# One token block through attention, gated linear attention and pooling: where turned sums, a diagonal, a table load and two copies stand

## The reference, cut to what matters

```python
def first_block(x, ...):
    for l in range(DEPTH):                       # two layers
        h = rmsnorm(x, attn_norm_g[l])
        proj = h @ w_in[l]
        qa, ka, va, ga, cq, ckv, kr, gb = jnp.split(proj, SPLIT_POINTS, axis=-1)
        ya = swa_attention(...) * jax.nn.silu(ga)        # 16 heads, window 128
        yb = mla_attention(cq, ckv, kr, ...) * jax.nn.silu(gb)   # 8 heads, low-rank q and kv
        x = x + jnp.concatenate([ya, yb], axis=-1) @ w_out[l]
    return rmsnorm(x, final_norm_g)

def second_block(x, c, ctx, c_ctx, w_ada, ...):
    for i in range(DEPTH):
        sh, sc, gt = modulation(c_lat, w_ada[i], b_ada[i], 3)    # silu(c) @ w + b
        u = x * (1.0 + sc) + sh
        if i % 2 == 0:
            sh_c, sc_c = modulation(c_c, w_ada[i], b_ada[i], 2)
            uc = ctx_s * (1.0 + sc_c) + sh_c
            s_f, s_b = context_states(uc @ w_in_e[j][:, :E_STATE_COLS], ...)
            y, _, _ = even_mixer(u @ w_in_e[j], s_f, s_b, ...)   # 4 heads of gla_chunked, both directions
        else:
            y = odd_mixer(u @ w_in_o[j], w_pool[j], ...)
        x = layer_norm(alpha * x + gt * y, ln_g[i], ln_b[i])

def gate_log(r, w, b):
    return jax.nn.log_sigmoid((r @ w + b).astype(jnp.float32)) / GLA_TAU

def gla_chunked(q, k, v, log_a, s0):             # one head: decayed scores, decayed state
    g = jnp.cumsum(lac, axis=-2)
    decay = jnp.exp(jnp.where(lower, diff, -jnp.inf))
    scores = jnp.einsum('bhik,bhjk,bhijk->bhij', qc, kc, decay)
    o = (jnp.einsum('bhij,bhjv->bhiv', scores, vc)
         + jnp.einsum('bhik,bhkv->bhiv', qc * jnp.exp(g), s))
```

## Time and profile before

| what | value |
|---|---|
| three timed runs | 1691.81, 1695.49, 1695.62 us, median 1695.49 |
| the profiled execution's own time | 1694.16 us |
| its span, first to last instruction | 1692.4 us |
| PE busy | 1653.7 us, 98% |
| DVE busy | 1348.3 us, 80% |
| ACT busy | 903.3 us, 53% |
| transfers | 390.59 MB, mean 231 GB/s |
| granted TensorE clock, mean | 0.993 |

### The profile page before, as it was taken

One profiled execution on the slowest core, in us unless ns is written; L12 is line 12 of the kernel. 1 busy time (PEld: TensorE's weight loads), 2 busy tenths in 40 slices (PEclk: granted clock), 3 DMA queues, 4 the chain that ended last, 5 costly groups with the idle time before them and its releaser, 6 DMA issues.

```text
span 1692.4 us, 22024 instructions
## 1 busy us (share of the span) xinstructions
PE 1653.7 (98%) x7948; PEld 1372.3 (81%) x7948; DVE 1348.3 (80%) x1761; ACT 903.3 (53%) x1352; POOL 155.2 (9%) x222
## 2 busy tenths in 40 slices
PE   9999999999999999998999999999999999999996
PEld 8888888888888888786877878888877778888885
DVE  6988878879978878787975787778877978777766
ACT  6447564445475644655843466666534364444432
POOL 1100000001100000011211110000101101110000
PEclk9999999999999999999999999999999999999998
DMA  8965545658755546789987963434959869887663
GB/s 325 329 237 187 175 162 161 216 189 297 275 165 185 182 154 208 262 277 315 336 270 227 304 206 125 132 129 166 322 179 346 306 233 318 284 271 237 224 206 112
DMA packets 111409, 390.59 MB, mean 231 GB/s; under 512 B 16252, under 2 KB 17164, under 8 KB 109804
## 3 DMA queue, kind: packets, MB, share of 16 engines
q1 hardware_dynamic: 74944, 268.99, 45.6%
q0 software_dynamic: 27856, 101.19, 19.5%
q10 hardware_dynamic: 8510, 19.08, 3.2%
HBM read 385.02 MB, written 4.19 MB: 230 GB/s over the span
## 4 chain that ended last, share of the span: by engine, by line
PE 82%; DVE 7%; DMA 5%; ACT 3%; issue 2%; POOL 0%; ACTq 0%; DVEq 0%; SPq 0%; POOLq 0%
PE L L392 22%; PE L L393 22%; PE L L399 22%; DMA stage<-in_w_stream 5%; PE TP L505 3%; DVE wl L334 2%; PE AB L2506 2%; DVE macc L678 2%; PE AB L2203 1%; ACT wh L313 1%; PE TP L2216 1%; PE AB L2522 1%; PE AB L2440 1%; PE AB L2206 1%; PE AB L2229 1%
## 5 line engine op out<-in xcount | busy, mean ns | idle before, releaser
L392 PE MATMUL L<-wh,xth 128*128 128x512 f32 (+1 forms) x1948 | 783.6, 402 | 3.6 <-issue 2.7
L313 ACT ACTIVATE wh<-stage 128x1024 fp32r<-128x1024 f32 x504 | 530.5, 1057 | 476.2 <-PE L L399 336.4
L334 DVE TENSOR_TENSOR wl<-stage,wh 128x1024 fp32r<-128x1024 f32 x504 | 612.6, 1221 | 210.4 <-ACT wh L313 209.5
L393 PE MATMUL L<-wh,xtl 128*128 128x512 f32 (+1 forms) x1948 | 761.0, 391 | 0.0
L399 PE MATMUL L<-wl,xth 128*128 128x512 f32 (+1 forms) x1948 | 524.2, 390 | 1.8 <-DVE wl L334 1.7
L399 PEld LDWEIGHTS L<-wl,xth 128*128 128x128 f32 x1948 | 366.6, 188 | 79.5 <-DVE wl L334 3.1
L392 PEld LDWEIGHTS L<-wh,xth 128*128 128x128 f32 x1948 | 367.6, 189 | 77.5 <-issue 5.3
L393 PEld LDWEIGHTS L<-wh,xtl 128*128 128x128 f32 x1948 | 367.8, 189 | 73.5 <-issue 2.4
L678 DVE SCALAR_TENSOR_TENSOR macc<-mstage,scols,macc 128x1024 f32<-128x1024 f32 x240 | 306.9, 1279 | 7.3 <-DMA mstage<-in_w_mod 6.6
L745 POOL DMA_DIRECT2D mstage<-in_w_mod x192 | 138.9, 724 | 1256.4 <-DVE macc L678 1014.2
L815 ACT ACTIVATE pa<-pa,st 128x128 f32<-128x128 f32 x96 | 43.0, 450 | 67.9 <-DVE st L1403 37.4
(11 more groups left out here) (262 smaller groups left out, 1322.6 us busy)
## 6 DMA issues: line engine op xcount, KB each, us to landing
stage<-in_w_stream SPq DMA_DIRECT2D x504, 512.0 KB, 4.5
mstage<-in_w_mod POOLq DMA_DIRECT2D x192, 512.0 KB, 6.0
arena<-in_ctx ACTq DMA_DIRECT2D x1, 2048.0 KB, 9.4
x_kept<-X ACTq DMA_DIRECT2D x4, 512.0 KB, 7.5
X<-x_kept ACTq DMA_DIRECT2D x1, 2048.0 KB, 10.5
arena<-in_b_ada ACTq DMA_DIRECT2D x2, 1024.0 KB, 10.9
arena<-in_ln_g ACTq DMA_DIRECT2D x2, 1024.0 KB, 10.1
X<-in_x SPq DMA_DIRECT2D x3, 512.0 KB, 8.3
```

Of the source, the lines that this page charges most:

```text
L313: nc.scalar.activation(wh[:, s % SPLITS].rearrange("p a b -> p (a b)"), stage[:, s % RING, :], ACT.Copy).then_inc(hi_ready, 1)
L334: nc.vector.tensor_tensor(wl[:, s % SPLITS].rearrange("p a b -> p (a b)"), stage[:, s % RING, :], wh[:, s % SPLITS].rearrange("p a b -> p ...
L392: nc.tensor.matmul(dst[:, t, 0:width], xh, w, start=start and k == 0, stop=False, skip_group_check=True)
L393: nc.tensor.matmul(dst[:, t, 0:width], xl, w, start=False, stop=False, skip_group_check=True)
```

## The change

Seven places are touched; all of them change the order of work, and no product of the reference is computed otherwise.

1. In the last 16 slots of an attention layer PE turned x behind slots 6, 8, 10, 12 and the sums behind 7 and 9. Now x stands behind 6, 10, 14, 15 and the sums behind 8 and 12. ACT and DVE follow (8, 12, 16, 17; sums 10, 14).
2. The turned sums of the context stretch, behind its slot 23 before, stand behind the third latent slot and its gate. DVE's reductions move along. Two waits of PE on `mod_cols` go.
3. `head_gates(0)` stands behind the query slot 10, not 9; ACT's three steps on it and DVE's `decay_logs(0)` stand one step later too.
4. The first head's diagonal is summed by ACT behind the first level's exponentials and not ahead of slot step 4.
5. A one-element exponential on ACT stands between slot steps 4 and 5 of each head.
6. The first emptying of the low-rank query group waits for the third slot's first half alone (`first_queries`), not for the whole slot.
7. ACT's rounding of a gate row (`gate_row_high(0, 0)`, L963) stands behind one more slot copy.

```diff
@@ evac, evac_q: ACT in an attention layer
-                    slots_done(act, N0 + done)
+                    if done:
+                        slots_done(act, N0 + done)
+                    else:
+                        act.wait_ge(once("first_queries"), l + 1)
...
-                        evac_q(0, MIDQ + 3)
+                        evac_q(0, None)
@@ step: PE, third low-rank query slot
                                 last = products(L[(G0 + G_MIDQ + k) % 2], n % SPLITS, k, 2, False, lx)
+                                if k == 0:
+                                    last.then_inc(once("first_queries"), 1)
@@ last 18 steps of a layer: ACT
-                    if n in (8, 10, 12, 14):
-                        turn_x(l + 1, (n - 8) // 2)
+                    if n in (8, 12, 16, 17):
+                        turn_x(l + 1, (8, 12, 16, 17).index(n))
@@ the same: DVE
-                    if n in (8, 10, 12, 14):
-                        turn_x(l + 1, (n - 8) // 2)
-                    if n in (9, 11):
-                        mod_unit(1, (n - 9) // 2)
+                    if n in (8, 12, 16, 17):
+                        turn_x(l + 1, (8, 12, 16, 17).index(n))
+                    if n in (10, 14):
+                        mod_unit(1, (n - 10) // 4)
@@ the same: PE
-                    if n in (7, 9):
-                        turn_unit(1, (n - 7) // 2)
-                    if n in (6, 8, 10, 12):
-                        turn_x(l + 1, (n - 6) // 2)
+                    if n in (8, 12):
+                        turn_unit(1, (n - 8) // 4)
+                    if n in (6, 10, 14, 15):
+                        turn_x(l + 1, (6, 10, 14, 15).index(n))
@@ context stretch: DVE (on ACT "if n == 27: u.n += 2" goes, and u.n += 4 becomes 6)
-                if n == 27:
-                    mod_columns(dve, 4, 0, [u.take()[1], u.take()[1]], 2, 1, KT, True)
...
+                if n == 2:
+                    mod_columns(dve, 4, 0, [u.take()[1], u.take()[1]], 2, 1, KT, True)
@@ context and latent stretch: PE
-                if p == 23:
-                    turn_sums(0, 4, 0, [u.take()[1], u.take()[1]])
...
-                if j == 1:
-                    pe.wait_ge(mod_cols, MOD_COLS[5])
...
-                turned(pe, len(TURNS) + 2 + m + 1)
+                turned(pe, len(TURNS) + m + 1)
                 kv_step(m)
                 log_gate(m)
+                if m == 2:
+                    turn_sums(0, 4, 0, [u.take()[1], u.take()[1]])
...
-            pe.wait_ge(mod_cols, MOD_COLS[6])
@@ query stretch: PE; ACT's decay steps move from 10, 11, 12 to 11, 12, 13, DVE's from 13 to 14
-                if n == 9:
+                if n == 10:
                     low_rank_ready(2)
                     head_gates(0)
@@ a head's start: ACT
+                def diagonal_sums():
                     ...
+                if hd:
+                    diagonal_sums()
+                split_step(act, split_hi, R_G, HEAD_STEPS * hd + 4)
+                nc.scalar.activation(st[:, 52:53], ones[:, 0:1], ACT.Exp)
+                split_step(act, split_hi, R_G, HEAD_STEPS * hd + 5)
...
+                    if hd == 0 and v == 0:
+                        diagonal_sums()
@@ behind the heads: ACT
-            gate_row_high(0, 0)
-            split_pairs(act, split_hi, R_G + BESIDE, 1, evac_to(6144, 0, 1024))
+            split_pairs(act, split_hi, R_G + BESIDE, 1, evac_to(6144, 0, 1024),
+                        beside=lambda i, n: gate_row_high(0, 0) if n == 0 else None)
```

More of the change, by code:

```diff
@@ L999, in _ @@
                     keep_x((n - 24) // 4)
-                if n == 27:
-                    u.n += 2
                 if n >= 28:
@@ L1064, in _ @@
             z_uses = []
-            u.n += 4
+            u.n += 6
             def decay_abs(hd):
@@ L1091, in beside_q @@
                     low_rank_high(2)
-                if n == 10:
+                if n == 11:
                     decay_abs(0)
-                if n == 11:
+                if n == 12:
                     decay_exp(0)
-                if n == 12:
+                if n == 13:
                     decay_ln(0)
@@ L1122, in _ @@
                     split_step(act, split_hi, R_G, HEAD_STEPS * hd + n)
-                act.wait_ge(once("diagonal"), hd + 1)
-                for j in range(TT):
-                    d = pa[:, 1024 + GD * j:1024 + GD * j + GD]
-                    ins = nc.scalar.activation(d, d, ACT.Copy, accum_out=st[:, 54 + j:55 + j])
-                ins.then_inc(once("diagonal_sum"), 1)
-                for n in (4, 5):
-                    split_step(act, split_hi, R_G, HEAD_STEPS * hd + n)
+                def diagonal_sums():
+                    act.wait_ge(once("diagonal"), hd + 1)
+                    for j in range(TT):
+                        d = pa[:, 1024 + GD * j:1024 + GD * j + GD]
+                        ins = nc.scalar.activation(d, d, ACT.Copy, accum_out=st[:, 54 + j:55 + j])
+                    ins.then_inc(once("diagonal_sum"), 1)
+                if hd:
[3 more added lines that the diff above has]
+                split_step(act, split_hi, R_G, HEAD_STEPS * hd + 5)
                 for v, b in enumerate(LEVELS + [128]):
@@ L1674, in beside_q @@
                     gates_to_rows(2)
-                if n == 13:
+                if n == 14:
                     decay_logs(0)
```

## The result

The changed kernel took 1677.95 us (median of 4 runs, 1674.28 to 1678.49), the kernel before 1693.78 beside it (4 runs, 1691.81 to 1695.62). The ratio is 0.9906, with a 95% interval of 0.9886 to 0.9926: faster by 15.8 us, where 14.9 were forecast, and 1677.95 lies 1.6 us under the forecast 1679.5 and inside the range. A later comparison gave 0.9913 (0.9896 to 0.9929). The profiled execution took 1678.49 us, its span is 1676.7.

What follows compares the result with a forecast made beforehand. PE was taken as the bound, busy 1653.7 of 1692.4 us, leaving 38.7 us idle. Terms 6.3 + 2.2 + 1.8 + 3.5 + 0.8 + 0.3 = 14.9 from 1694.16 give 1679.3; forecast 1679.5 us, range 1672 to 1688.

Steps and rivals of the forecast that it cites:

- What bounds: Whole kernel: PE busy 1653.7 of 1692.4 us, so 38.7 us idle to win back; seven places touched, weight-stream slots stay.
- Item 1: Context stretch, turned sums: waits of 1.27 and 4.62 plus 2.4 of clock go, bank wait of 2.0 comes; 6.3 us.
- Rival (a): Context stretch gives little, its removed waits having served the weight stream: 2 instead of 6.3 us, time 1683.6; chance 0.12.
- Rival (c): Context stretch slower: turned latent tiles wait for blocks landing over 10 us after issue; 25 us lost, 1704; chance 0.04.
- Item 2: Ends of the two attention layers: waits of 0.81 and 1.62 go, about 0.2 new in the second; 2.2 us.
- Items 3 and 4: First head's gates and start: 1.67 wait goes, 2.1 bank wait comes, 1.76 and 0.5 gained; 1.8 us together.
- Item 5: Heads two to four, exponentials' table loaded ahead: DVE paces levels, shift 1.28 each; 3.5 us, 0.2 with a drain.
- Items 6 and 7: Gate row behind the heads, 0.8 us of a 0.95 wait; low-rank queries' emptying in the layers, 0.3 us.
- Rival (b): The two new bank waits, in the context stretch and before q's tiles, do not come; time 1675.2; chance 0.13.
- (d): Change lacks its effect: heads as before, first head's start and table load ahead near zero; 1684.6; chance 0.07.
- (e): Gains and new waits cancel: context stretch and first head's gates at lower ends, half the table-load gain; about 1690; chance 0.06.
- signs of being wrong: Half clock anywhere else before the last products, PE waiting at more than one latent tile, or a head as long as before.

Runs made afterwards that it cites:

- edit 3 back: The changed kernel with the first head's gates behind slot 9 again, ACT's three steps and DVE's logarithms one slot earlier: 1677.02 us.

## Why the prediction was right, by its steps

**What bounds.** Right. PE's instructions stayed, and the gain is idle time and clock; the seven places were the right seven.

**Item 1**, 6.3 against 6.8 here and 7.95 when undone. The mechanism stands: both waits and the fall of the clock go, and a bank wait comes, 1.93 against 2.0. The 0.5 is the clock's term: 1.27 + 4.62 - 1.93 leaves 2.9 of the 6.8 for it where 2.4 was taken, and 6.8 us at half clock are two stretches of 1.43. The cause of the new wait was half seen. I worked DVE's time from its queue alone; that queue begins when the stream lets it. Rival (a) was right that the transfers fill the stretch, wrong that they therefore take the gain. Rival (c) named blocks later than 10 us after issue: they were 12.9, but only one tile paid. In 7 of the 10 traces with this wait it was 2.47 to 3.55 us and the clock fell behind it, at its place 1.9 to 3.1 us more than in the changed kernel, and the half clock around 790 that should have been gone was there. In both traces of the changed kernel it was not. That 1.93 met the 2.0 is in part luck.

**Item 2**, a term too small: 2.2 against 2.6 to 3.3. The 0.2 put down for a new wait in the second layer did not come, and each end gave 0.3 to 0.6 us more than its wait was long (1.4 for 0.81, 1.9 for 1.62), for which the sum had no term.

**Items 3 and 4**, 1.8 against 1.75, with both parts right: -0.4 against -0.6, and 2.3 against 2.35. But the first head's 2.35 can't be put down to the diagonal's new place alone. In the changed kernel undoing it costs 0, and undoing the load ahead costs 1.38. The other 0.97 is a difference of two measurements and no run shows whose it is; the kernel before lacks the wait of 2.27 as well, and without that wait ACT's slot copy would stand behind POOL's product again, as the times with edit 3 back suggest. Item 4 didn't see that the bank wait of item 3 gives POOL time.

**Item 5**, 3.5 against 4.2, with "3.8 at most". The step that failed is the pace: "DVE sets the levels' pace", and PE gains on it. It is a loop of ACT and DVE, entered at the first level, so a late start of the loop is paid in full at the last level, 1.37 to 1.42 a head where PE waited 0.5. The number is 1.41 and not 1.28: the exponentials start 2.38 us after the last slot copy's start with the load between (1029.74 to 1032.12) and 0.97 with it ahead (1121.11 to 1122.08), since an activation starts 0.09 before the copy ends and the load does not. The one element itself lies in idle time. The prediction's 0.2 for item 5 in case of a drain would not have followed either: that drain would have gone from in front of the exponentials too.

**Items 6 and 7**, 0.8 against 0.97, and 0.3 against 0. A wait of 0.16 us on a weight load cost PE's matmuls nothing: by the modelled ends they were still working off the loads ahead (until 164.78 in that kernel, the load at 164.54).

The terms erred by +0.5, +1.1, 0, +0.7 and -0.2, and the start and the tail of that execution by -1.3, so the near hit of 14.9 against 15.7 is partly luck. Rival (b) is out, since both new waits came; (d) and (e) are out, since the heads and the moved waits gave what they should. Of the signs of being wrong, none came in the changed kernel's own traces: its low clock is behind the heads, where the kernel before had it, and only one latent tile waits.

## What to carry to other kernels

Before removing a wait, ask which buffer the waiting work would next want back and who frees it; here two of the seven places got a new wait of about 2 us, one as large as the wait removed, and moving the freeing step one slot earlier brought 2.55 us where the edit itself had brought nothing. Where two engines hand work to and fro in a loop, add up the loop's steps, not the work of one engine: a step beside the loop can be cut at no gain, and a late entry is paid in full. And compare kernels by the same piece of work in both traces: the spans here scattered by more than most terms, while the places of two traces of one kernel agreed to 0.2 us over the first 377 slots.

## What the runs showed of the hardware

- A wait of 2.27 us, the same to 0.01 in eleven traces, was followed by the lower of TensorE's two levels, 1.2 GHz, in three of them (3.4 us, some 1.5 lost) and not in the others, though PE's four slots before it were alike in all, 2.72 us each. A wait of 2.67 us near the end, the same in all fourteen traces, came with it in ten. At the context stretch a wait of 1.93 us or less never did, one of 2.30 or more always.
- A releaser can be wrong where two engines end within some 10 ns of each other.
- Blocks of 512 KB that land 4.6 us after their issue by the program's median took 12.9 where three queues loaded together, at a DMA share of 1.0; the same three blocks took 12.8 in the changed kernel's second trace, and 12.3 to 14.3 in those of other kernels.
